# Final residual written in the row order of the experts, with the routing beside the last projection and the closing steps by halves

## The reference

```python
x = x + y @ w_out                      # y: the gated sum of the two branches
h = rmsnorm(x, ffn_norm_w)
g_prob = softmax(h @ w_group + b_group)             # 8 groups: the best one is taken
e_sel = (h @ w_expert + b_expert)[the best group]   # 8 experts of it: the best two
x = x + sum over a token's two experts e of
        weight_e * ((silu(h @ w1[e]) * (h @ w3[e])) @ w2[e])
out = rmsnorm(x, final_norm_w)
```

## Time and profile before

| | us |
|---|---|
| median of three runs | 1672.27 |
| the profiled execution | 1672.93 |
| its span | 1671.1 |
| TensorE busy | 1490.6 |
| VectorE busy | 617.0 |
| ScalarE busy | 526.5 |
| DMA, bytes read | 493.93 MB |

### The profile page before, as it was taken

How to read it: one execution, slowest core, us unless ns; L and a number is a source line. 1 busy time by engine, 2 the same in 40 slices (tenths; PEclk the granted TensorE clock), 3 DMA queues, 4 the chain that set the end, 5 groups by cost and what they waited for, 6 DMA issues and landing times.

```text
span 1671.1 us, 20396 instructions
## 1 busy us (share of the span) xinstructions
PE 1490.6 (89%) x8555; PEld 889.7 (53%) x8555; DVE 617.0 (37%) x1375; ACT 526.5 (32%) x1117; POOL 0.2 (0%) x4
## 2 busy tenths in 40 slices
PE   7998999898999999879999998888888888888886
PEld 5785878577787788744444443333333333333332
DVE  6666566455755566541121211211211211112112
ACT  5666466556554565421111111111111111111101
POOL 0000000000000000000000000000000000000000
PEclk9999899889999999978999999999999999999998
DMA  7242243233413445779999999999999999999995
GB/s 271 101 151 101 101 139 125 77 126 120 152 57 104 148 152 206 264 310 403 428 427 427 428 427 427 427 428 428 427 427 426 429 427 426 428 427 427 429 426 222
DMA packets 74562, 496.36 MB, mean 297 GB/s; under 512 B 6208, under 2 KB 10592, under 8 KB 49504
## 3 DMA queue, kind: packets, MB, share of 16 engines
q1 hardware_dynamic: 74464, 495.00, 72.7%
HBM read 493.93 MB, written 1.05 MB: 296 GB/s over the span
## 4 chain that ended last, share of the span: by engine, by line
PE 60%; DMA 26%; DVE 7%; ACT 5%; issue 1%; SPq 0%; DVEq 0%; ACTq 0%
DMA arena<-in_expert_w 26%; PE ps L1044 20%; PE ps L1377 8%; PE ps L1369 8%; PE ps L1419 5%; PE ps L1399 4%; DVE arena L1881 3%; PE ps L1041 2%; PE ps L1352 2%; ACT arena L1470 2%; PE ps L1140 1%; ACT arena L1473 1%; PE ps L1024 1%; DVE w_lo L1881 1%; PE ps L1075 1%
## 5 line engine op out<-in xcount | busy, mean ns | idle before, releaser
L1878 DVE COPY arena<-ps 128x512 f32<-128x512 f32 (+2 forms) x196 | 116.8, 596 | 630.7 <-PE ps L1369 478.2
L1369 PE MATMUL ps<-arena 128*32 128x512 f32 x2048 | 252.3, 611 | 54.1 <-DMA arena<-in_expert_w 53.1
L1881 DVE TENSOR_TENSOR w_lo<-arena,w_hi 128x512 fp32r<-128x512 f32 (+2 forms) x304 | 199.8, 672 | 133.1 <-ACT w_hi L1473 131.4
L1473 ACT ACTIVATE arena<-ps 128x512 f32<-128x512 f32 (+6 forms) x243 | 121.0, 500 | 388.6 <-PE ps L1369 207.3
L1377 PE MATMUL ps<-arena 128*128 128x512 f32 x512 | 239.9, 612 | 0.0
L1473 ACT ACTIVATE w_hi<-arena 128x512 fp32r<-128x512 f32 (+2 forms) x320 | 192.9, 620 | 101.7 <-PE ps L1044 88.7
L1470 ACT ACTIVATE arena<-ps 128x128 f32<-128x128 f32 (+2 forms) x140 | 48.9, 373 | 459.0 <-PE ps L1399 431.2
L1369 PEld LDWEIGHTS ps<-arena 128*32 128x32 f32 x2048 | 56.4, 110 | 243.4 <-issue 116.3
L1044 PE MATMUL ps<-w_hi,hT_hi 128*128 128x512 f32 (+3 forms) x448 | 176.6, 394 | 5.9 <-DVE w_lo L1881 3.6
L1377 PEld LDWEIGHTS ps<-arena 128*128 128x128 f32 x512 | 93.4, 192 | 151.3 <-issue 151.3
L1044 PE MATMUL ps<-w_lo,hT_hi 128*128 128x512 f32 (+3 forms) x448 | 168.7, 377 | 0.0
(11 more groups left out here) (154 smaller groups left out, 1432.5 us busy)
## 6 DMA issues: line engine op xcount, KB each, us to landing
arena<-in_expert_w SPq DMA_DIRECT2D x192, 2048.0 KB, 30.9
arena<-in_w_in SPq DMA_DIRECT2D x23, 2048.0 KB, 7.8
arena<-in_w_out SPq DMA_DIRECT2D x6, 2048.0 KB, 8.1
arena<-in_w_in SPq DMA_DIRECT2D x3, 1536.0 KB, 6.6
arena<-in_w_mem_kv SPq DMA_DIRECT2D x2, 2048.0 KB, 9.1
arena<-in_w_branch_hgrn SPq DMA_DIRECT2D x2, 2048.0 KB, 7.9
arena<-in_w_branch_mla SPq DMA_DIRECT2D x2, 2048.0 KB, 8.2
arena<-in_mla_w_uq SPq DMA_DIRECT2D x2, 1152.0 KB, 5.5
```

Source lines behind the costliest of these rows:

```text
L1369: o = e.matmul(B[32 * j:32 * j + 32, :], Xs[:, k, q:q + 32], Wn[:, k, :], start=i == 0, stop=i == 1)
L1473: return e.activation(o, i, ACTF.Copy, scale=scale)
L1878: return e.tensor_copy(o, i)
L1881: return e.tensor_tensor(o, a, b, op)
```

## The change

Seven edits belong together (in the diff, `scales` and the flag's block are TensorE's, `half is not None` is ScalarE's split, `preceding` and the lines on `XS`, `s8`, `gmx` and `emx` are VectorE's, `m == 1` is in SyncE's `expert`, and the last lines are GpSimd's).

1. `w_out_2` is loaded as two sets of rows (k-blocks 0 to 3 and 4 to 7), each over all 1024 columns, and a piece takes of each run of 8 columns the lower or upper 4.
2. Two VectorE copies ("order") write `x`, permuted, to `xk` in steps of the stage before; the residual is added there, so the sum is already in the experts' order and not normalized.
3. Turns of the first half of `xk` and half of the logits' products are put between the pieces of the last projection half. The upper parts `g_hi` are ScalarE copies, and the lower parts `g_lo` are made by GpSimd, which had no work before.
4. The norm is applied later: to the logits, and to the gathered rows by a matrix `R`, which TensorE makes for each group of eight experts with two float32 matmuls of 256 columns (`scales`). VectorE does all gathered copies, where ScalarE did half.
5. The choice is found by comparing all pairs of eight (`preceding`) and not by three maxima.
6. The router and norm weights have new places and wait for nothing; the order of the slots and the waits of expert matrices 1 to 3 are new.
7. The last w2 comes in two halves of columns with a semaphore each; down, combine, sum, squares and output of the last expert are done by halves, and the flag is read earlier.

```diff
+    for k in (0, 4):
+        out.append(("fold", rows(A["w_out_2"][0])[:, k:k + 4, :], 4, 1024, None))
...
+    last = len(uses) - 2
+    parts += [(last + k // 4, k % 4, 512, half) for half in range(2) for k in range(8)]
...
             if half == 0:
-                add("end", "om")
+                for t in range(2):
+                    after(1 + 2 * t, step("order", t))
         add("table")
...
+        chain((1, step("parts", 0, 0)), (1, step("parts", 0, 1)))
+        chain((1, turned), (2, logits))
+        bs = []
+        yield from mult(("y",), PAIR, bs, lambda k: ("yT", k // 2 * 2) in done)
+        add("residual", 2, 1, bs)
+        A, B = get(), get()
+        add("turn x", 4, A, B)
+        add("parts", 1, 0)
+        add("mean x")
+        add("take x", 4, B)
+        add("logits", 4, P.logits)
+        add("parts", 1, 1)
...
-        RING = [6, NU % 2, 1 - NU % 2, 2, 3, 4, 5]
+        RING = [6, 4, NU % 2, 1 - NU % 2, 2, 3, 5]
...
+            def scales(g):
+                B = banks[3][:, 0:256] if g == 0 else B7[:, 256:512]
+                w.wait_ge(*at("reach"))
+                if g:
+                    w.wait_ge(*at("x", g - 1, 7))
+                for t in range(2):
+                    w.wait_ge(*at("oh", "g", g, t))
+                    i = e.matmul(B, reach[:, t, :], OH[:, t].bitcast(F32).rearrange("p e s -> p (e s)"), start=t == 0, stop=t == 1)
+                i.then_inc(mark(pe_x, ("in r", g)), 1)
...
+                if g < 7:
+                    if ex % 8 == 0:
+                        scales(g + 1)
                     gather(g + 1, 0, ex % 8)
...
+                if ex == NE - 1:
+                    w.wait_ge(*at("flag"))
+                    over = e.value_load(flagi[0:1, 0:1])
+                down(ex, 0)
+                if ex == NE - 1:
+                    combine(ex, 0)
+                down(ex, 1)
+            combine(NE - 1, 1)
...
+                    if half is not None:
+                        o = copy(in_runs(RW[q % NRW][0][:, 0, :], 4), in_runs(slot_of(u)[:, kp, :], 8)[:, :, 4 * half:4 * half + 4])
...
+            def preceding(v8, o):
+                d4 = pairs.rearrange("p (t e f) -> p t e f", t=2, e=8)
+                w.wait_ge(*book.newest)
+                tt(d4, bc(v8, 2, 8), bc(v8, 3, 8), ALU.subtract).then_inc(mark(dve_route), 1)
+                w.wait_ge(*book.newest)
+                tt(d4, d4, bc(c("tie").rearrange("p (e f) -> p e f", e=8), 1, 2), ALU.is_ge).then_inc(mark(dve_route), 1)
+                w.wait_ge(*book.newest)
+                total(o, d4, ALU.add).then_inc(mark(dve_route), 1)
...
+                stt(XS[g % 2][:, k, :], B, p("gffn")[:, k:k + 1], R, ALU.mult, ALU.mult).then_inc(mark(dve_moe, ("x", g, k)), 1)
...
+            ts(s8, before_e, 1.5, None, ALU.is_lt).then_inc(mark(dve_route), 1)
+            total(gmx, gl, ALU.max).then_inc(mark(dve_route), 1)
+            total(emx, es, ALU.max).then_inc(mark(dve_route), 1)
...
+                elif m == 1:
+                    w.wait_ge(*at("y", 1))
+                elif m < 4:
+                    w.wait_ge(*at(*plan.ends[NU - 4 + m]))
...
+                    e.tensor_tensor(glo[:, t, cs], xk[:, t, cs], ghi[:, t, cs].bitcast(F32), ALU.subtract).then_inc(
+                        mark(pool_lo, ("glo", half, t)), 1)
```

More of the change, by code:

```diff
@@ L202, in order_of_work @@
     P.scores = {}
-    kinds = [(u[0], u[2], u[3]) for u in uses]
-    queue, cursor, later, done = deque(), [0, 0], [], set()
+    P.logits = None
+    parts = []
+    for u, (kind, _, k, n, _) in enumerate(uses):
+        if kind == "split":
+            parts += [(u, q, n, None) for q in range(k)]
+        elif kind == "whole":
+            parts.append((u, None, n, None))
+    last = len(uses) - 2
+    parts += [(last + k // 4, k % 4, 512, half) for half in range(2) for k in range(8)]
+    final = {u: i for i, (u, *_) in enumerate(parts)}
+    queue, cursor, later, done = deque(), [0], [], set()
     def after(n, fn):
@@ L771, in ends, with turned, logits @@
             if half == 0:
-                add("end", "om")
+                for t in range(2):
+                    after(1 + 2 * t, step("order", t))
         add("table")
[L774 to L778, removed]
+        bs = []
+        yield from mult(("y",), PAIR, bs, lambda k: ("yT", k // 2 * 2) in done)
+        add("residual", 2, 0, bs)
+        put(*bs)
+        def turned():
+            if len(P.pool) < 2:
+                return False
+            A, B = get(), get()
+            add("turn x", 0, A, B)
+            add("take x", 0, B)
+            put(A, B)
+        def logits():
+            P.logits = get()
+            add("logits", 0, P.logits)
+        chain((1, step("parts", 0, 0)), (1, step("parts", 0, 1)))
+        chain((1, turned), (2, logits))
+        bs = []
+        yield from mult(("y",), PAIR, bs, lambda k: ("yT", k // 2 * 2) in done)
+        add("residual", 2, 1, bs)
+        A, B = get(), get()
+        add("turn x", 4, A, B)
[4 more added lines that the diff above has]
+        add("parts", 1, 1)
     run(ends())
     add("end", 2)
-    assert not later and not queue and cursor[0] == len(kinds)
+    assert not later and not queue and cursor[0] == len(parts)
     return P
@@ L1700, in scalar @@
                         w.wait_ge(*at("new x", l, half, t))
-                        run(hn[:, t, cs], x[:, t, cs], ACTF.Square, accum_out=squares[:, 2 * half + t:2 * half + t + 1]).then_inc(
+                        run(ntb[t] if l == 2 else oG[:, t, cs], (xk if l == 2 else x)[:, t, cs], ACTF.Square,
+                            accum_out=squares[:, 2 * half + t:2 * half + t + 1]).then_inc(
                             mark(act_norm, ("squares", l, half, t)), 1)
+                elif kind == "parts":
+                    half, t = s
+                    cs = slice(half * 512, half * 512 + 512)
+                    w.wait_ge(*at("new x", 2, half, t))
+                    copy(ghi[:, t, cs], xk[:, t, cs]).then_inc(mark(act_moe, ("ghi", half, t)), 1)
+                elif kind == "mean x":
+                    root("late", 2, "row", 3)
                 elif kind == "bounds":
```

425 lines of the change are left out of this document (233 added, 192 removed).

## The result

The changed kernel took **1677.94 us** (median of 18 runs, 1675.09 to 1683.87) against **1672.25** for the kernel before (18 runs, 1669.66 to 1675.54): a ratio of **1.0032 [1.0023, 1.0041]**, slower by 0.3%, which is clear of the noise. The forecast was 1669.5, with a range of 1664.5 to 1675. The profiled execution took 1678.65 us, with a span of 1676.9; before it was 1672.93 and 1671.1, so the two profiles differ by as much as the medians (5.7).

The account below looks back on a forecast made before the run. DMA flow of expert matrices was taken as the bound from matrix 12 on; matrix 12 issued 1.5 us earlier and the end 1.3 shorter gave -2.8 from 1672.27, so 1669.5 us, range 1664.5 to 1675.

Parts of the forecast that it names:

- (a): Last projection: piece 4 now needs use 42, second half of w_out_2, before needed at piece 8; +2.9 us, bounds 0 and +7.3.
- (b): Between the last half's projection pieces: eight transposes, a wait for the residual, eight of 16 logit products; +3.4 us.
- (c): From the residual's end to the last logit: 3.3 us where there were 11.6; -8.3 us.
- (d): Choice of experts: 13 small operations at 0.25 us instead of 22; -1.7 us.
- (e): Counts to first gather: a subtraction and count product go, two float32 products come; +0.5 us (0.2 to 1.1).
- (f): Gather to first up product: products wait only for their own rows, clock granted sooner; -1.4 us (-0.8 to -3).
- first expert: After the first up product: VectorE's chain +1.9, TensorE's products and copy of R +1.8, faster clock -0.6; +3.1 us (0.5 to 5).
- the end: After the last matrix: last expert by halves, fewer additions left, narrower squares, earlier flag; -1.3 us (-3 to +1).
- dear bound: Upper bound of (a): use 42 lands at 684.4 as before, +4.9, and ScalarE's four splits cost +2.4; +7.3 us.
- rival 3: Slower projection: the stall at (a) is 7.3 us and not 2.9; 1673.9 us, chance 0.09.
- rival 2: Root and choice: VectorE stands still while GpSimd makes the last two g_lo, 1.3 us each; 1672.1 us, chance 0.11.
- rival 4: Expert groups: TensorE becomes the bound, six or seven groups with 2.3 us more each; 1685 us, chance 0.05.

Follow-up runs that it names:

- e1: Changed kernel with the second half of w_out_2 (use 42) issued ahead of the router and norm weights; 1676.15 us, 1.0022 to the kernel before.
- e2: Changed kernel with g_lo made by VectorE and GpSimd idle; 1676.82 us, 1.0034 to the kernel before.
- e9: Changed kernel with GpSimd's last two g_lo waiting for the choice; 1680.45 us in one run.
- e5: Changed kernel with use 42 ahead of small loads, g_lo on VectorE, first expert's weights later and table earlier, new end; 1667.04 us, 0.9974 to the kernel before.
- e10: Changed kernel with only a new end: both last down products before combines, branch earlier, weighing on GpSimd, squares on ScalarE; 1675.67 us, 1.0020 to the kernel before.
- e3: Changed kernel with the end of the kernel before; 1677.49 us, 1.0037 to the kernel before.
- e4: Changed kernel without the fallback and the branch over it, on every engine; 1678.57 us, 1.0041 to the kernel before.
- e8: Changed kernel with both halves of the last down product issued ahead of their combines; 1677.58 us in one run.
- e6: Changed kernel, own end kept, with use 42 ahead of small loads, g_lo on VectorE, first expert's weights later and table earlier; 1672.41 us, 0.9998 to the kernel before.

## Why the prediction was wrong

Step by step, from the two profiles (after minus before, us):

| step | predicted | measured |
|---|---|---|
| (a) wait for `w_out_2`, and the clock after it | +2.9 | +7.2 |
| (b) work put between | +3.4 | +2.8 |
| (c) residual to last logit | -8.3 | -8.3 |
| (d) choice | -1.7 | -0.1 |
| (e) counts to gather | +0.5 | +0.4 |
| (f) gather to first up | -1.4 | -1.6 |
| first expert | +3.1 | +4.0 |
| second expert | 0 | -0.9 |
| from matrix 12 to the last down product | 0 | +2.4 |
| the end | -1.3 | +1.5 |
| stages ahead | 0 | -1.5 |
| sum | -2.8 | +5.8 |

**(a) is the step that failed most**, and with it the choice between its bounds. I put use 42's issue at 673.5 and its landing at 682.3 (11.9 and 20.7 us after the zero) on the ground that SyncE would be free early. But the norm weights, moved with the others, held SyncE 11.1 us, so the load went 13.2 us after expert matrix 0 and took 9.5 us, both as before. From the landing on my working held: 1.4 us for the split and 2.7 for the branch. That is the landing of my dear bound and of rival 3, to which I gave 0.09; it moved the turn by 4.8 us, against 4.9 in that bound. Rival 3's time, 1673.9, is still 4 us short. The rest of that bound's 7.3 came from elsewhere: ScalarE's splits of runs of four columns cost 0.63 as all others, and the 2.4 us were TensorE at half its clock after the gap. I had priced the wait for the weights and not the clock after it. e1, in which use 42 goes 11.8 us after the zero, shows the order of the loads to be worth 5.0 of the 7.2 by its profile at the residual's end, and 4.3 at the first up product.

**(d)** was 1.6 us too low: one is GpSimd's (e2, e9), so rival 2's mechanism is real at 1.0 us and not the 2.6 I priced it at; the rest is wider operations, 0.3 us each for 128 columns where I had put 0.25 for all. **(b), (c), (e) and (f)** held to 0.6 us.

**First expert:** 0.9 too low. VectorE's chain was as I made it: the hidden turn that waits for it starts 7.8 us after the first up product's start, where it was 6.1, so +1.7 against +1.9. That turn then ran at the low clock and took 1.91 us in place of 1.08, which I had not counted (0.8). From its end to the gather were 5.2 us in place of 3.0, so +2.3 where I had +1.8 for `R`. The down product gave back 0.8, against 0.6. In e5, with the eight products and ScalarE's table load moved out of this path, the stage is 2.2 shorter.

**The flow** from matrix 12 on held to 1 us: the last landing moved with it, 892.7 us after matrix 12's issue and not 891.7. TensorE did not become its bound (rival 4): the stretch from 850 to 1000 moves 427 GB/s, against 428. But the last down product waits for TensorE's work behind the landing of the last w1, and not for the last landing, and that work took 11.7 us where it took 10.0:

```profile
1646.63 2.56 PE L1436 MATMUL ps<-arena 128*32 128x512 f32 x16 [2.74 <-DMA arena<-in_expert_w]
1649.12 4.72 PE L1443 MATMUL ps<-arena 128*128 128x512 f32 x8
```

These took 1.92 and 3.70 us in the kernel before; the granted clock was 0.78 from 1645 to 1650 and 0.88 from 1650 to 1655, where it was 1.00 in both. In e10, where TensorE's work is the same up to there, the same two take 1.92 and 3.70 behind a wait of 2.76 us. So 1.7 of the row's 2.4 us are what one execution happens to get: from the end of the second down product to the last down product's start e3, e4, e9 and the changed kernel, in which both rows ran slow, have 894.4 to 895.3 us, and e8 and e10, in which they did not, 893.1 and 892.3.

**The end:** 2.8 us too low. TensorE's part was as forecast (+1.9). From its end to the last addition's I counted 0.7 us and it took 1.2. From there to the first output block I took 1.1 off for narrower squares and an earlier flag, and it took 0.8 more (4.6 against 3.8): I gave the branch no price, and here 2.24 us of it stand open (e4), where 0.99 did. From the first block to the span's end I took 0.4 off, and it took 5.3 us in both.

The edits measured one at a time do not add up in the ratios: e1's 4.3 us of profile (2.6 per mille) gave 1.0 per mille of ratio, and the mended front and end together gave 5.8 per mille. What I call shown are the rows, and by e6 that mending the front alone takes back as much as the change lost; how the loss in time divides among the steps is not shown.

## What to carry to other kernels

When work that needs a load is moved earlier, ask first what stands ahead of that load in its queue, the issue times of the small ones too, and put the load that is needed first in front. The length of an issue in a profile may be a wait and no price: ask what landed when it ended (here 2.75 us became 11.11). A gap of TensorE can be paid for twice, in waiting and in the clock after it: the one of 4.63 us was (2.4 us more), e1's of 1.77 was not. And where an idle engine takes over work, look for the engine with which it cannot run at once, and count what a shorter chain uncovers at its end: branches, and reads in a changed order.

## What the runs showed of the hardware

- SyncE's issue of a 512 KB load that repeats one row over 128 partitions took 2.75 us in the kernel before, 2.81 in e1 and 11.11 in the changed kernel. In all thirteen kernels it ended 0.25 to 0.51 us before the landing of the last 2 MB load issued ahead of it.
- Two-input VectorE operations beside GpSimd's subtraction: 1.93 us for two of two columns (0.35 without it), 1.81 for two of 256 (0.76). GpSimd needs 1.26 to 1.72 us for 128x512, VectorE 0.64. For rival 2 an estimate of 1.1 us had been worked out from the Trainium skill ("GPSIMD Engine Reference", Performance versus the Vector engine), a little under the measured ones.
- A branch over a block that is not run left VectorE 2.24 us without work in the changed kernel (gone in e4), 0.99 in the kernel before and none in e3, where 3.80 us of additions stand ahead of it.
- An addition of 128x512 with one operand in PSUM took 0.62 us with both in the same order and 0.95 to 1.0 with one permuted. ScalarE's 128x512 splits took 0.63 in either order.
